# Reading the tokens of every projection product backwards, and writing its bank backwards

## The reference

```python
q, k, v = jnp.split(hn @ w_qkv_a[layer], 3, axis=-1)
h = h + o @ w_o_a[layer]
kv = _rmsnorm(h, norm_kv) @ w_kv
return (jax.nn.silu(h @ w_gate) * (h @ w_up)) @ w_down
proj = jnp.einsum('bsd,de->bse', h, w_in[l])
y_a = jnp.einsum('bsc,cd->bsd', y_a, w_short_out[l])
a, bgate = jnp.split(jnp.einsum('bsd,df->bsf', h2, w_ffn_in[l]), 2, axis=-1)
```

## Time and profile before

| | us |
|---|---|
| median of two runs | 2050.95 |
| the two runs | 2049.29, 2052.61 |
| span of the profiled execution | 2050.8 |
| TensorE matmuls busy (PE) | 2016.6 |
| weight loads busy (PEld) | 1645.1 |
| VectorE busy (DVE) | 1066.4 |
| ScalarE busy (ACT) | 798.3 |
| GpSimd busy (POOL) | 629.0 |

### The profile page before, as it was taken

One profiled execution on the slowest core, in us unless ns is written; L12 is line 12 of the kernel. 1 busy time (PEld: TensorE's weight loads), 2 busy tenths in 40 slices (PEclk: granted clock), 3 DMA queues, 4 the chain that ended last, 5 costly groups with the idle time before them and its releaser, 6 DMA issues.

```text
span 2050.8 us, 28727 instructions
## 1 busy us (share of the span) xinstructions
PE 2016.6 (98%) x9556; PEld 1645.1 (80%) x9556; DVE 1066.4 (52%) x1445; ACT 798.3 (39%) x1182; POOL 629.0 (31%) x416
## 2 busy tenths in 40 slices
PE   7999999999999999999999999999999999999997
PEld 5777788888887777788888888888888888888886
DVE  6666644343465666544343456699855552332324
ACT  5545443342253444454332354222227352222224
POOL 1111255341134333246341254444444031001013
PEclk9999999999999999999999999999999999999999
DMA  4122244443234344244443332233323323333333
GB/s 155 62 72 82 83 143 166 162 144 102 92 112 93 82 84 111 77 140 174 151 146 99 95 123 73 94 101 92 102 92 93 102 83 99 95 95 100 92 102 103
DMA packets 64036, 218.80 MB, mean 107 GB/s; under 512 B 7792, under 2 KB 9968, under 8 KB 63856
## 3 DMA queue, kind: packets, MB, share of 16 engines
q1 hardware_dynamic: 60912, 213.96, 32.8%
q0 software_dynamic: 3072, 4.20, 1.6%
HBM read 211.83 MB, written 2.10 MB: 104 GB/s over the span
## 4 chain that ended last, share of the span: by engine, by line
PE 92%; DVE 3%; issue 2%; ACT 1%; POOL 1%; DMA 1%; DVEq 0%; SPq 0%; ACTq 0%; POOLq 0%
PE G L1524 28%; PE G L1526 28%; PE G L1525 28%; PE Z L1648 2%; PE O L1666 2%; PE Z L1629 2%; PE Z L1524 1%; PE Z L1526 1%; PE Z L1525 1%; DVE ez L940 0%; DVE sp L923 0%; DMA raw<-stream 0%; DVE Z L1053 0%; PE O L1675 0%; DMA qkv<-tmp 0%
## 5 line engine op out<-in xcount | busy, mean ns | idle before, releaser
L375 ACT ACTIVATE wh<-raw 128x1024 fp32r<-128x1024 f32 x338 | 358.5, 1061 | 970.0 <-PE G L1526 957.5
L1524 PE MATMUL G<-xh,wh 128*128 128x512 f32 (+1 forms) x1616 | 634.0, 392 | 10.3 <-DVE xl L835 9.5
L1525 PE MATMUL G<-xl,wh 128*128 128x512 f32 (+1 forms) x1616 | 626.9, 388 | 0.0
L1526 PE MATMUL G<-xh,wl 128*128 128x512 f32 (+1 forms) x1616 | 626.9, 388 | 0.0
L806 DVE TENSOR_TENSOR wl<-raw,wh 128x1024 fp32r<-128x1024 f32 x277 | 385.5, 1392 | 180.8 <-ACT wh L375 177.6
L1524 PEld LDWEIGHTS G<-xh,wh 128*128 128x128 f32 x1616 | 304.0, 188 | 82.8 <-issue 15.0
L1524 PE MATMUL G<-yh,wh 128*128 128x512 f32 x904 | 352.1, 389 | 3.8 <-POOL yl L1420 2.1
L1526 PEld LDWEIGHTS G<-xh,wl 128*128 128x128 f32 x1616 | 303.9, 188 | 63.3
L1525 PEld LDWEIGHTS G<-xl,wh 128*128 128x128 f32 x1616 | 304.2, 188 | 61.6 <-issue 1.0
L1526 PE MATMUL G<-yh,wl 128*128 128x512 f32 x904 | 350.6, 388 | 0.0
L1525 PE MATMUL G<-yl,wh 128*128 128x512 f32 x904 | 350.5, 388 | 0.0
(11 more groups left out here) (245 smaller groups left out, 1970.5 us busy)
## 6 DMA issues: line engine op xcount, KB each, us to landing
raw<-stream SPq DMA_DIRECT2D x340, 512.0 KB, 3.5
araw<-ada_w SPq DMA_DIRECT2D x48, 512.0 KB, 4.3
fraw<-stream SPq DMA_DIRECT2D x8, 512.0 KB, 4.7
qkv<-tmp POOLq DMA_DIRECT2D x64, 64.0 KB, 4.0
h<-x_t SPq DMA_DIRECT2D x8, 256.0 KB, 6.8
out_t<-h SPq DMA_DIRECT2D x16, 128.0 KB, 1.8
con<-const_d SPq DMA_DIRECT2D x1, 1344.0 KB, 10.3
cs<-c_row SPq DMA_DIRECT2D x1, 512.0 KB, 4.2
```

The source lines that it names most:

```text
L375: eng.activation(wh[s][:, :, :], raw[s][:, :, :], ACT.Copy).then_inc(w_hi, 1)
L1524: eng.matmul(total, hi[:, k, :], src_h[:, k, cols], start=k == 0, stop=False)
L1525: eng.matmul(total, hi[:, k, :], src_l[:, k, cols], start=False, stop=False)
L1526: mm = eng.matmul(total, lo[:, k, :], src_h[:, k, cols], start=False, stop=k == kt - 1)
```

## The change

Both sides of each of the three matmuls are given with a step of minus one: the moving operand is read from its last token to its first, and the result is written into the bank from its last column to its first. Every result therefore lands at the same address as before. The stationary operand, the number of instructions, their order, the semaphores and the readers of the banks are as before. In a product of half the tokens the half is reversed in itself. No other matmul is touched.

```diff
@@ -1521,9 +1521,10 @@
                         eng.wait_ge(ready[k % 2], before // 2 + k // 2 + 1)
                     else:
                         eng.wait_ge(ready, before + k + 1)
-                    eng.matmul(total, hi[:, k, :], src_h[:, k, cols], start=k == 0, stop=False)
-                    eng.matmul(total, hi[:, k, :], src_l[:, k, cols], start=False, stop=False)
-                    mm = eng.matmul(total, lo[:, k, :], src_h[:, k, cols], start=False, stop=k == kt - 1)
+                    back_h, back_l = src_h[:, k, cols][:, ::-1], src_l[:, k, cols][:, ::-1]
+                    eng.matmul(total[:, ::-1], hi[:, k, :], back_h, start=k == 0, stop=False)
+                    eng.matmul(total[:, ::-1], hi[:, k, :], back_l, start=False, stop=False)
+                    mm = eng.matmul(total[:, ::-1], lo[:, k, :], back_h, start=False, stop=k == kt - 1)
                     if k == kt - 1 and done is not None:
                         mm.then_inc(done, 1)
```

## The result

The changed kernel takes 2096.66 us, the median of two runs (2096.50 and 2096.83), against 2050.95: 45.7 us more, ratio 1.0222 (95% interval 1.0192 to 1.0252). Timed again in more rounds it is 2097.55 against 2050.88 us, ratio 1.0225 (1.0211 to 1.0239). It is slower, by a little over 2%; the first interval alone would still have left room for less than 2%.

The account below looks back on a forecast made before the run. TensorE was taken to bound the kernel, busy for 98% of the span, so product-matmul distances go into the time almost one for one. All terms were zero: 2050.8 + 0, forecast 2051 us, 8-in-10 range 2040 to 2163.

Parts of the forecast that it names:

- its likeliest case: Three product matmuls: no change in the distance between starts, 2051 us, with its own range of 2044 to 2058; chance 0.66.
- a dearer start: Rival: every descending matmul pays more than the fixed 13.3 ns; 2051 to 2163 us, 2% reached at 4.9 ns; chance 0.13.
- a doubling of the fixed part: Upper bound of a dearer start: the 13.3 ns of each product matmul doubles, 112 us more, 2163 us.
- The prediction's own sign of failure: The forecast falls if the distance at 512 columns differs from 0.2267 us by 5 ns or more.
- The count of 7992 and 432 matmuls: Product matmuls on the three lines: 7992 of 512 columns and 432 of 256, 8424 in all.
- the split of 2050.8 us: All products 1863 us, 91% of the span; remaining 188 us scores, transposes, weighted sums, PE's waits, start and end.
- Half rate: Rival: the descending read or bank write takes one column in two periods; +1751 us, 3802 us; chance 0.17.
- the rate of the reversed stream: Step on product operands with step minus one: bounded between 1939 and 3802 us, taken as no change, 0 us.
- the pairs and the groups of four are the same in either direction: Reason for 0 us: the same 512 neighbours are read, so the number of memory groups is unchanged.
- 213.3 ns of columns and 13.3 ns that don't depend on their number: Split of the 0.2267 us between 512-column product matmuls, from 0.2267 us at 512 and 0.120 at 256 columns.
- weight loads cost what they did: Term for instructions, waits and queues: the stationary side keeps its direction, so its loads add nothing.
- What I said a dearer start would look like: Sign in the changed profile: the same added nanoseconds per product matmul at 512 and at 256 columns.

Follow-up runs that it names:

- bench of places: TensorE alone, without the kernel: 74 sections of 36 identical fp32r matmuls, weights and tokens at varied offsets; 512 columns forward: 226.7 ns at a=0, 233.5 at a=16.
- shift by 64 bytes: Against the kernel before, all reads forward: wh and wl lie 64 bytes higher behind an unused row; 2096.07 us, ratio 1.0220.
- the bench: At the bank's write: TensorE alone, 49 sections of varied sizes and directions, 226.7 ns with only the write backward; at 228.7, 233.5 and 236.7 ns, the bench of places.

## Why the prediction was right or wrong

The forecast of 2051 us, its likeliest case at 0.66, was wrong; the time fell into the rival "a dearer start", inside the range, and just beyond the 2% that I had put at 4.9 ns a matmul: 45.7 us / 8424 is 5.4. That the range holds the time is luck in good part: its upper end was a doubling of the fixed part, for which I had no reason, and the rival's mechanism isn't what the runs show. The prediction's own sign of failure, a distance 5 ns or more away from 0.2267 us, came true with 6.7.

*What held.* PE sets the time, and a changed distance goes into it almost one for one: 49.2 us of distance became 43.9 us of span. (One reading was loose: the chain gives the product matmuls 28 + 28 + 28 and 3%, that is 87% of the span, not the 91% with which I said it agrees.) The count of 7992 and 432 matmuls and the split of 2050.8 us held. No instruction was added, no wait arose, nobody waited for columns, the clock stayed. Half rate didn't come. The bank's write cost nothing, as I had said.

*The step that failed* is the rate of the reversed stream, where the prediction says "I take nothing": measured, it is 6.7 ns a matmul at 512 columns. The reason given, that the pairs and the groups of four are the same in either direction, doesn't carry it: groups of 4 backwards keep every 16 bytes in upward order and cost as much as single elements (2096.75 us), and only with groups of 64 is the cost gone (2051.29 us; in the bench of places groups of 32 have 232.7 ns, of 64 and 128 226.7). Under it lies "213.3 ns of columns and 13.3 ns that don't depend on their number", taken as a constant of every matmul, together with "weight loads cost what they did", taken as if the load and the moving read had nothing to do with each other. The 13.3 ns are what a forward fp32r read of 512 columns pays, with a weight load beside it, when the two lie alike modulo 256 bytes; out of place it is 15 to 23 ns, backward 20 to 23, and 2.5 in bf16 (215.8 less 213.3) and in plain fp32 (429.2 less 426.7). The weight load's address alone, with the moving read untouched, moves the distance (places bench, shift by 64 bytes). The Trainium skill (TensorE: Matmul & The Clock Gate, Part 2, the step on LDWEIGHTS) says that the next weights' load takes no read bandwidth from the running matmul, thanks to a port of its own; for bf16 no run here speaks against it; for fp32r the place of the weights changes the pace of the matmuls, which doesn't fit the sentence, though no run shows where the two meet.

*The rows of before had said so.* I used to count and passed over their durations: 394 and 391 ns for x and y with wh, but 414 for x2h (some of it because it often stands behind other work) and 402 for fwh, at equal shape and type. The timeline of before at the fwh products, which I didn't look at, has three matmuls in 0.70 us, 0.2333 each, without any backward read:

```profile
220.32 0.40 PE L1525 MATMUL Z<-yl,fwh 128*128 128x512 f32 x1
220.55 0.39 PE L1526 MATMUL Z<-yh,fwl 128*128 128x512 f32 x1
220.78 0.40 PE L1524 MATMUL Z<-yh,fwh 128*128 128x512 f32 x1
221.02 0.39 PE L1525 MATMUL Z<-yl,fwh 128*128 128x512 f32 x1
```

By the sizes of the buffers ahead of them, the rows of x2h begin 64 bytes off those of wh modulo 256, and those of fwh 64 bytes off those of yh, while xh, yh and wh agree. The bench gives 228.7 and 233.5 ns for these two offsets; the trace of before had 229.9 and 233.3. A distance that differs by buffer is not a constant, and a change to a buffer's access could then have been priced from the dearest of those rows: 7992 x 6.7 ns is some 53 us, near the result. That would have been an estimate and no bound (the bench has 236.7 ns at some places), and that a backward read costs what a misplaced one does is a finding of the runs, not of the rows of before.

*What I said a dearer start would look like*, the same nanoseconds at 512 and 256 columns, is wrong as well: 6.3 more at 512; at 256 it is 1.4 less with wh/wl and 3.4 more with fwh/fwl. By that test I would have called the result neither of my cases.

*Why 44 us of span and not 53.* The kernel before didn't run at 226.7 ns everywhere: its fwh products had 233.3, its x2 products 229.9, and behind each piece of other work the forward products take about a dozen matmuls to settle. In the trace of before, over the 77 stretches of x and y products, the first three distances average 233.4, 232.8 and 232.5 ns, the eleventh 226.8, and from there on they average 226.7. Backward products run at 233.2 to 233.6 from the second on, so there they lost less. Together these take about 4.5 us off the 53, and the shorter waits of PE 3.6; 1.7 us stay unaccounted for, as said.

*Open.*
## What to carry to other kernels

Before pricing a change to an operand's access, compare the distance between starts of equal matmuls that differ only in their buffers: if it varies, the "fixed" part isn't fixed, and the dearest row is a better first price than nothing (53 us here, against 46 measured). For fp32r products of 512 columns at the engine's limit, let the weights' and the moving operand's rows agree modulo 256 bytes, both at a multiple of 32 bytes, and read forwards, or backwards by blocks of at least 64 elements; a stray 64 bytes of padding costs as much as a reversed read, 2.2% here. At 256 columns neither holds: forward, backward, in place or out of it, the distances are 116 to 120 ns. The bank may be written in either direction for nothing.

## What the runs showed of the hardware

- fp32r, 512 columns, at 2.4 GHz: 226.7 ns from start to start with weights and tokens alike modulo 256 bytes (230.0 when both are moved by 16 bytes), 229 to 237 ns otherwise, 233.3 backward (235.6 to 236.7 at b=1, 2 and 32). bf16: 215.8 forward and backward, at every place tried.
- fp32r, 256 columns: 120 ns forward, 118 backward; with the weights moved by 64 bytes 116 forward.
- The write of a bank backwards: no cost (2050.49 against 2050.88 us; 226.7 ns in the bench).
- A moving fp32r operand with a step of 2 elements: 453 ns, half rate; with a step of minus one it is 233 ns. In bf16 a step of 2 costs 10 ns (225.8).
- Weights of 64 or 32 columns make forward matmuls slower, not faster: 230.0 and 231.7 ns for 226.7.
